# The head-pair loop rotated, and buffers moved to multiples of 512 bytes, in a two-layer decoder trunk

## The chip, the core and the metric

The kernel runs on one core of a Trainium2 chip. The metric is the device time of one launch in microseconds (us), as the median of several runs. A profile is one execution, taken by the hardware profiler. Its engines are PE (TensorE matmuls), PEld (TensorE weight loads), DVE (VectorE), ACT (ScalarE), POOL (GpSimd) and SP (SyncE, which here issues the DMAs).

## What is computed

`x` has 512 tokens of 1024 channels in float32. Each of two layers computes two token mixers from one projection, merges them, and adds a squared-ReLU MLP:

```python
def hybrid_layer(x, g_mix, w_in, w_a, w_b, w_o, g_ffn, w_up, w_down):
    proj = rmsnorm(x, g_mix) @ w_in
    qa, ka, va, qr, kr, vr, gr, ga, gb = jnp.split(proj, SPLIT_POINTS, axis=-1)
    # A: softmax attention, 8 heads of 64 in 3 groups of dilation 1, 4, 16; partial rotary;
    #    the groups' outputs are combined by their softmax denominators
    y_a = combine(outs, lses) @ w_a
    # B: retention, 4 heads of key dim 128 and value dim 256, full rotary, decay per head
    ret = retention(rotary(qr), rotary(kr), vr)
    ret = ret * lax.rsqrt(jnp.mean(ret * ret, axis=-1, keepdims=True) + NORM_EPS)
    y_b = (jax.nn.silu(gr) * ret) @ w_b
    x = x + (sigmoid(ga) * y_a + sigmoid(gb) * y_b) @ w_o
    return x + jnp.square(jax.nn.relu(rmsnorm(x, g_ffn) @ w_up)) @ w_down
```

A last RMSNorm follows the second layer.

## The kernel before

**Units.** All weights stream through SBUF in units of 1 MB (512 KB for a `w_a` unit). SP loads a unit into `raw[s]` as two DMAs, ACT rounds it to `w_hi` (line 393, called by `ahead`), DVE subtracts to get `w_lo` (line 683, `lo`), and PE multiplies. There are two slots of each buffer. To reach float32 precision, activations are also kept as `_hi` and `_lo` parts, and each product is three matmuls in fp32r format (lines 1075 to 1077): `w_hi` by hi, `w_hi` by lo, `w_lo` by hi. A normal unit is two output tiles `o` (PSUM banks `pj[0]`, `pj[1]`) of 8 contraction steps `k`: 48 matmuls that each stream 512 columns of the activation past 128 columns of weights. A `w_a` unit has 4 steps and so 24 matmuls.

**A layer** has 82 units:
- 6 value units (lines 1124 to 1126), in which the activation is the stationary side and 512 columns of weights stream: 288 matmuls in a layer;
- 24 units of the head-pair loop: 4 pairs of 6 units. Units 0 to 2 are queries and keys of the three attention groups, unit 3 those of retention, unit 4 the retention values (lines 1234 to 1236: 96 matmuls that stream 256 columns of weights), unit 5 the swish gate;
- 16 units of `gates(p)`, p = 0 to 3: gate A and gate B (activation `h`), `w_b` (activation `z_hi`, `z_lo`), `w_a` (activation `y_hi`, `y_lo`);
- 4 units of `w_o` (activation `m_hi`, `m_lo`);
- 32 units of the MLP: 16 with activation `h_hi`, `h_lo`, and 16 with `u_hi`, `u_lo`, which are the `z_hi`, `z_lo` buffers again.

So over both layers 88 units of 48 matmuls stream `h` (4224), and 2496 matmuls stream z, m or y: 1920 from `z`, 384 from `m`, 192 from `y`. The attention and retention products themselves are plain fp32 matmuls.

**Places of the buffers.** `x`, `h_hi`, `h_lo`, the raw and split weights follow one another from where the framework's constants end, byte 16512 of each partition. Their sizes are multiples of 2048, so each starts 128 bytes past a multiple of 512. The zone behind the fixed buffers starts at the next multiple of 64, byte 131648, which is 64 bytes past a multiple of 512; `z`, `U`, `m_hi`, `m_lo`, `z_hi`, `z_lo`, `y_hi`, `y_lo`, `ST`, `prob` and others lie in it, all 64 past.

**The pair loop.** PE does units 0 to 2 of the pair, then 12 steps `s` of half a tile of units 3 to 5, with pieces of the attention and retention between them: `scores(j)`, `turn(b)` (transposes of the probabilities), `values(b)`, `st(j)`, `ret(e)`. Each `b` goes PE scores, DVE `masked`, ACT `exp`, PE `turn`, ACT `probT_out`, PE `values`. At the end come `ret(1)` and one matmul by ones, whose result ACT takes the root of (line 544) and DVE inverts (line 856) before it scales two tiles of `z` (lines 861, 864). Only behind these does DVE's queue go on with the next pair: `lo` of its unit 1, then `rotary` (lines 766 to 775) of its units. `rotary` for unit 3 is placed among `masked`. ACT copies each query or key tile from PSUM (`rot_in`, line 465, 467 to 469), which frees the bank; POOL multiplies it by the cosine (line 663).

**After the last pair** PE does `gates(0)`: unit gate A, unit gate B, then `turn_two(0)`, which transposes `U` and waits for `u_scale(0)` and `u_scale(1)` on DVE (line 907), then the `w_b` unit, which waits for each split part of `z`. DVE's order there is `lo`, `gate(0,0,0)`, `factors` (lines 887 to 899), `u_scale(0)`, `u_scale(1)`, `gate(0,0,1)`, and only then the splits of `z` (line 869) and the rest. Each engine runs its own instructions in the order written; all the order between engines is by semaphores.

Of the kernel before, what the change touches and what calls it, by code (L numbers as in the profile page):

```python
# [35 lines left out]
P = 128  # L36
F32 = mybir.dt.float32
# [14 lines left out]
def trunk(nc, a):  # L52
# [30 lines left out]
    with ExitStack() as ctx:  # L83
# [9 lines left out]

        x = sb("x", [P, KT, S], F32)
# [8 lines left out]
        decay = sb("decay", [P, S], F32)  # L103
        mask = sb("mask", [P, S], F32)
        ident = sb("ident", [P, P], F32)
        ones = sb("ones", [P, P], F32)
        inv_d = sb("inv_d", [P, 1], F32)
        gains = sb("gains", [P, 2 * DEPTH + 1, KT], F32)
        gain = sb("gain", [P, 2, KT], F32)
        std = sb("std", [P, 2 * TB], F32)  # L110
        rstd = sb("rstd", [P, 2 * TB], F32)
        eps = sb("eps", [P, 1], F32)

        stats = sb("stats", [P, 2 * TB, 2, HEADS], F32)
        other = sb("other", [P, 2 * TB, 2, HEADS], F32)
        tick = sb("tick", [P, 1], F32)
        warm = sb("warm", [P, 1], F32)


        zone0 = -(-nc.sbuf_base // 64) * 64  # L120
# [24 lines left out]
        nmax = at("P", "nmax", [P, 2 * TB, 2], F32)  # L145
        den = at("P", "den", [P, 2 * TB, 2], F32)
# [7 lines left out]
        y_lo = at("G", "y_lo", [P, KA, S], F32R)  # L154
        sA = at("G", "sA", [P, 2, S], F32)
        sB = at("G", "sB", [P, 2, S], F32)
# [22 lines left out]
        rb = ps("rb", S)  # L179

# [205 lines left out]
        def _(act):  # L386
# [56 lines left out]
            with act.Fori(0, DEPTH) as l:  # L443
# [7 lines left out]
                with act.Fori(0, PAIRS) as i:  # L451
                    J = l * PAIRS + i
                    n = l * LU + P0 + i * P_U
                    q = banks(l, P0, P_U, i, 0)

                    def tile(u, o):
                        act.wait_ge(mm_done, (n + u) * 2 + o + 1 + MM_CREDIT)

                    def rot_in(u, o):

                        t = 2 * u + o
                        tile(u, o)
                        act.wait_ge(rot_out, J * 8 + t + 1)
                        if u < GROUPS:
                            nc.scalar.copy(rot[:], pj[o][:]).then_inc(bank_free[o], 1)  # L465
                        else:
                            nc.scalar.copy(rot[:], pj[o][:])
                            nc.scalar.copy(swp[0:64, :], pj[o][64:128, :])
                            nc.scalar.copy(swp[64:128, :], pj[o][0:64, :]).then_inc(bank_free[o], 1)

                    def exp(b):

                        for side in range(2):
                            act.wait_ge(att_masked, (J * 8 + b) * 2 + side + 1)
                            c, at_ = keys(side, b), side * TB + b // 2
                            nc.scalar.activation(prob[:, c], prob[:, c], ACT.Exp, scale=-1.0,  # L476
                                                 bias=nmax[:, at_, b % 2:b % 2 + 1],
                                                 accum_out=den[:, at_, b % 2:b % 2 + 1]).then_inc(att_exp, 1)

                    def probT_out(b):  # L480
                        act.wait_ge(att_turned, J * 8 + b + 1)
                        if b >= 1:
                            act.wait_ge(att_pv, J * 8 + b)
                        c = slice(keys(0, b).start, S)
                        nc.scalar.copy(probT[:, c], pt[:, c]).then_inc(att_probT, 1)

                    for u in range(GROUPS):
                        ahead(l, P0, P_U, i, u)
                        rot_in(u, 0)
                        rot_in(u, 1)  # L490
                    ahead(l, P0, P_U, i, 3)
                    exp(0)
                    rot_in(3, 0)
                    probT_out(0)
                    exp(1)
                    probT_out(1)
                    exp(2)
                    ahead(l, P0, P_U, i, 4)
                    rot_in(3, 1)
                    probT_out(2)  # L500
                    exp(3)
                    probT_out(3)
                    exp(4)

                    def vR_out(o):
                        tile(4, o)
                        if o == 0:
                            act.wait_ge(ret_mm, J * 2 + 1 + 1)
                        for half in range(2):
                            b = 2 * o + half  # L510
                            mm = nc.scalar.activation(vR[:, b, :], pj[o][:, half * RV:(half + 1) * RV], ACT.Copy,
                                                      scale=rstd[:, b:b + 1])
                        mm.then_inc(bank_free[o], 1)

                    vR_out(0)
                    probT_out(4)
                    exp(5)
                    probT_out(5)
                    exp(6)
                    ahead(l, P0, P_U, i, 5)  # L520
                    vR_out(1)
                    probT_out(6)
                    exp(7)
                    probT_out(7)

                    def ret_square(e):
                        act.wait_ge(ret_out, J * 2 + e + 1)
                        nc.scalar.activation(sqR[e], rb[:],
                                             ACT.Square).then_inc(ret_sq, 1)

                    def gate_sig(o):

                        act.wait_ge(bank_free[o], q + 6 + BANK_CREDIT)
                        nc.scalar.activation(sigR[o], silu[:, o, :], ACT.Sigmoid).then_inc(g_sigmoid, 1)

                    sigR = [swp[:], prob[:, 0:S]]
                    sqR = [rot[:], probT[:, 0:S]]
                    ret_square(0)
                    gate_sig(0)
                    act.wait_ge(att_pv, J * 8 + 8)  # L540
                    ret_square(1)
                    gate_sig(1)
                    act.wait_ge(ret_mean, J + 1)
                    nc.scalar.activation(probT[:], rb[:], ACT.Sqrt, bias=eps[:], scale=1.0 / RV).then_inc(ret_std, 1)

# [9 lines left out]
                ahead(l, G0, G_U, 0, 0)  # L555
# [14 lines left out]
                gate(0, 0, 0)  # L570
                act.wait_ge(z_done, l * KT + KT)
                split_z(range(0, 4))
                gate(0, 0, 1)
                ahead(l, G0, G_U, 0, 1)
                split_z(range(4, 8))
# [92 lines left out]
        def _(dve):  # L668
# [60 lines left out]
            with dve.Fori(0, DEPTH) as l:  # L729
# [23 lines left out]
                with dve.Fori(0, PAIRS) as i:  # L753
                    J = l * PAIRS + i
                    n = l * LU + P0 + i * P_U
                    q = l * LQ + i * P_U

                    def rotary(u, o):

                        t = 2 * u + o  # L760
                        dve.wait_ge(bank_free[o], q + u + 1 + BANK_CREDIT)
                        if t == 0:
                            dve.wait_ge(tables_done, l + 1)
                        if u < GROUPS:
                            nc.vector.memset(tick[:], 0.0)
                            nc.vector.stream_shuffle(swp[:], rot[:], SHUFFLE).then_inc(rot_swap, 1)  # L766
                            dve.wait_ge(rot_swap, J * 6 + t + 1)
                        nc.vector.tensor_tensor(swp[:], swp[:], sinA if u < GROUPS else sinR,  # L768
                                                ALU.mult).then_inc(rot_sin, 1)
                        dve.wait_ge(rot_sin, J * 8 + t + 1)  # L770
                        dve.wait_ge(rot_cos, J * 8 + t + 1)
                        if u == 0:
                            nc.vector.tensor_tensor(qk[:, t, :], rcos[:], swp[:], ALU.add).then_inc(rot_out, 1)
                        elif u < GROUPS:
                            nc.vector.tensor_tensor(qk[:, t, :].rearrange("p (r m) -> p r m", r=4),
                                                    by_residue(rcos[:]), by_residue(swp[:]),
                                                    ALU.add).then_inc(rot_out, 1)
                        else:
                            nc.vector.tensor_tensor(qkR[:, o, :], rcos[:], swp[:], ALU.add).then_inc(rot_out, 1)

                    def masked(b):

                        for side in range(2):
# [594 lines left out]
```

## Time and profile before

| | us |
|---|---|
| median of 3 runs | 2015.46 (2014.9 to 2018.23) |
| the profiled execution's own time | 2016.15 |
| its span, first to last instruction | 2014.3 |
| PE busy | 1987.7 (99%) |
| PEld busy | 1656.1 (82%) |
| DVE busy | 1108.2 (55%) |
| ACT busy | 727.5 (36%) |
| POOL busy | 98.2 (5%) |
| mean DMA rate | 88 GB/s |

1.85 us of the profiled execution lie outside the span, and the median is 0.7 us below that execution. Matmuls are pipelined, and the ends of their rows are modelled, so the busy time of PE is no measure of its speed: the distance from the start of one matmul to the start of the next is.

### The profile page before, as it was taken

The numbers are of one execution on the slowest core, as the hardware profiler recorded it, in microseconds if no ns is written. First come the engines' busy times: TensorE is split into PE (matmuls) and PEld (weight loads), VectorE is DVE, ScalarE is ACT, GpSimd is POOL, SyncE is SP. The second block draws the span as 40 slices with busy tenths as digits, with TensorE's granted clock in tenths as the row PEclk, the third lists the DMA queues.
The fourth block names the chain that finished last, engine by engine and source line by source line (L and its number), as shares of the span: only waits on it lengthen the run. The fifth ranks groups of instructions, "written<-read, shape, count | busy, mean of one in ns | idle before, by whom it ended". The sixth has DMA issues, their size and how long they took to land.

```text
span 2014.3 us, 27151 instructions
## 1 busy us (share of the span) xinstructions
PE 1987.7 (99%) x9640; PEld 1656.1 (82%) x9640; DVE 1108.2 (55%) x1724; ACT 727.5 (36%) x1147; POOL 98.2 (5%) x71
## 2 busy tenths in 40 slices
PE   8999999999999999999999999999999999999999
PEld 7988888888888888888889888888888888888887
DVE  5466574747446635444635574757564565445355
ACT  4143535354223313223322534344432233223233
POOL 0010110200000000000001110202000000000000
PEclk9999999999999999999999999999999999999999
DMA  5321222212223233232333222213133323232321
GB/s 173 106 90 48 83 89 62 89 44 84 94 94 105 84 104 101 87 104 84 105 106 89 63 89 62 89 42 99 44 95 97 111 84 105 84 104 83 104 84 63
DMA packets 202544, 177.63 MB, mean 88 GB/s; under 512 B 8432, under 2 KB 192880, under 8 KB 202224
## 3 DMA queue, kind: packets, MB, share of 16 engines
q1 hardware_dynamic: 202192, 176.51, 27.8%
q8 instruction: 38, 0.62, 0.1%
q10 hardware_dynamic: 288, 0.28, 0.0%
q14 instruction: 26, 0.21, 0.0%
HBM read 174.54 MB, written 2.23 MB: 88 GB/s over the span
## 4 chain that ended last, share of the span: by engine, by line
PE 75%; DVE 14%; issue 7%; ACT 2%; POOL 1%; DVEq 0%; DMA 0%; ACTq 0%; POOLq 0%; SPq 0%
PE pj L1075 19%; PE pj L1077 19%; PE pj L1076 19%; DVE w_lo L683 4%; DVE swp L768 3%; PE yo L1184 2%; DVE swp L766 2%; PE rb L1210 2%; DVE probT L856 1%; PE pj L1234 1%; PE pj L1236 1%; PE pj L1235 1%; PE pt L1171 1%; PE sc L1124 1%; PE sc L1126 1%
## 5 line engine op out<-in xcount | busy, mean ns | idle before, releaser
L1075 PE MATMUL pj<-h_hi,w_hi 128*128 128x512 f32 x1408 | 558.2, 396 | 2.2 <-DVE sA L914 1.6
L1077 PE MATMUL pj<-h_hi,w_lo 128*128 128x512 f32 x1408 | 548.6, 390 | 0.0
L1076 PE MATMUL pj<-h_lo,w_hi 128*128 128x512 f32 x1408 | 548.4, 389 | 0.0
L393 ACT CAST w_hi<-w_raw 128x1024 fp32r<-128x1024 f32 x330 | 329.0, 1045 | 380.1 <-PE pj L1077 286.1
L683 DVE TENSOR_TENSOR w_lo<-w_raw,w_hi 128x1024 fp32r<-128x1024 f32 x330 | 404.4, 1267 | 82.7 <-ACT w_hi L393 82.0
L1075 PEld LDWEIGHTS pj<-h_hi,w_hi 128*128 128x128 f32 x1408 | 264.4, 188 | 61.8 <-DVE w_lo L683 5.5
L1077 PEld LDWEIGHTS pj<-h_hi,w_lo 128*128 128x128 f32 x1408 | 264.3, 188 | 56.1
L1076 PEld LDWEIGHTS pj<-h_lo,w_hi 128*128 128x128 f32 x1408 | 264.5, 188 | 54.9 <-issue 1.8
L1075 PE MATMUL pj<-z_hi,w_hi 128*128 128x512 f32 x640 | 252.6, 395 | 0.6 <-DVE sB L914 0.6
L1077 PE MATMUL pj<-z_hi,w_lo 128*128 128x512 f32 x640 | 252.2, 394 | 0.0
L1076 PE MATMUL pj<-z_lo,w_hi 128*128 128x512 f32 x640 | 252.2, 394 | 0.0
L978 DVE TENSOR_TENSOR x<-pj,x 128x512 f32<-128x512 f32 x80 | 55.2, 691 | 201.4 <-PE pj L1077 201.4
L663 POOL TENSOR_TENSOR rcos<-rot,tables 128x512 f32<-128x512 f32 x64 | 97.7, 1526 | 1307.1 <-ACT rot L465 1175.9
L1075 PEld LDWEIGHTS pj<-z_hi,w_hi 128*128 128x128 f32 x640 | 119.7, 187 | 30.3 <-issue 1.1
L1077 PEld LDWEIGHTS pj<-z_hi,w_lo 128*128 128x128 f32 x640 | 119.7, 187 | 29.8
L1076 PEld LDWEIGHTS pj<-z_lo,w_hi 128*128 128x128 f32 x640 | 119.7, 187 | 29.3
L992 DVE TENSOR_TENSOR relu<-relu,rstd_all 128x512 f32<-128x512 f32 x64 | 44.3, 692 | 90.4 <-ACT relu L607 89.8
L465 ACT COPY rot<-pj 128x512 f32<-128x512 f32 x48 | 28.2, 587 | 182.1 <-PE pj L1077 96.8
L476 ACT ACTIVATE prob<-prob,nmax 128x256 f32<-128x256 f32 (+1 forms) x128 | 62.4, 489 | 66.0 <-DVE nmax L790 65.6
L607 ACT ACTIVATE relu<-pj 128x512 f32<-128x512 f32 x64 | 38.3, 599 | 129.2 <-PE pj L1077 129.2
L1234 PE MATMUL pj<-w_hi,h_hi 128*128 128x256 f32 x256 | 79.4, 310 | 0.0
L790 DVE CUSTOM_DVE_ANT_0 prob<-sc,mask 128x256 f32<-128x256 f32 (+1 forms) x128 | 46.9, 404 | 56.6 <-issue 56.6
(185 smaller groups left out, 2358.1 us busy)
## 6 DMA issues: line engine op xcount, KB each, us to landing
w_raw<-in_w_in SPq DMA_DIRECT2D x152, 512.0 KB, 4.4
w_raw<-in_w_up SPq DMA_DIRECT2D x64, 512.0 KB, 4.4
w_raw<-in_w_down SPq DMA_DIRECT2D x64, 512.0 KB, 4.3
w_raw<-in_w_b SPq DMA_DIRECT2D x16, 512.0 KB, 4.0
w_raw<-in_w_o SPq DMA_DIRECT2D x16, 512.0 KB, 4.0
w_raw<-in_w_a SPq DMA_DIRECT2D x16, 256.0 KB, 3.0
x_nat<-in_x SPq DMA_DIRECT2D x2, 1024.0 KB, 7.0
tables<-in_tables SPq DMA_DIRECT2D x2, 1024.0 KB, 6.8
```

Source lines behind the costliest of these rows:

```text
L393: nc.scalar.copy(w_hi[s][:, c], raw[s][:, c]).then_inc(hi_done, 1)
L476: nc.scalar.activation(prob[:, c], prob[:, c], ACT.Exp, scale=-1.0, bias=nmax[:, at_, b % 2:b % 2 + 1], accum_out=den[:, at_, b % 2:b % 2 ...
L663: nc.gpsimd.tensor_tensor(rcos[:], rot[:], cosA if u < 3 else cosR, ALU.mult).then_inc(rot_cos, 1)
L683: nc.vector.tensor_tensor(w_lo[s][:, c], raw[s][:, c], w_hi[s][:, c], ALU.subtract).then_inc(lo_done, 1)
L768: nc.vector.tensor_tensor(swp[:], swp[:], sinA if u < GROUPS else sinR, ALU.mult).then_inc(rot_sin, 1)
L790: nc.vector.tensor_tensor_reduce(out=prob[:, c], in0=sc[:, (b % 2) * S + c.start:(b % 2) * S + c.stop], in1=mask[:, c], scale=-(DH ** -0.5 ...
L978: nc.vector.tensor_tensor(x[:, t, :], pj[o][:], x[:, t, :], ALU.add).then_inc(bank_free[o], 1)
L992: nc.vector.tensor_tensor(relu2[:, o, :], relu[:, o, :], rstd_all[:], ALU.mult).then_inc(relu_scaled, 1)
L1075: nc.tensor.matmul(out, w_hi[s][:, wc], acts[0], start=first, stop=False)
L1076: nc.tensor.matmul(out, w_hi[s][:, wc], acts[1], start=False, stop=False)
L1077: return nc.tensor.matmul(out, w_lo[s][:, wc], acts[0], start=False, stop=last)
L1234: nc.tensor.matmul(out, hh, w_hi[sl][:, w], start=(k == 0), stop=False)
```

## The change

**Places.** The small tensors move ahead of `x`, and a filler makes `x` start at a multiple of 512 bytes. The zone starts at a multiple of 512 too. `other` becomes a view of `decay`; `sB` and `sA` change places. All streamed operands now start at multiples of 512.

```diff
+        fill = -nc.sbuf_base % 512
+        if fill:
+            sb("fill", [P, fill // 4], F32)
         x = sb("x", [P, KT, S], F32)
...
+        other = decay[:, 0:2 * TB * 2 * HEADS].rearrange("p (b w h) -> p b w h", b=2 * TB, w=2)
...
-        zone0 = -(-nc.sbuf_base // 64) * 64
+        zone0 = -(-nc.sbuf_base // 512) * 512
...
+        sigR = [qkR[:, 0, :], prob[:]]
+        sqR = [qkR[:, 1, :], probT[:]]
```

**Order.** On each engine the loop over pairs becomes: queries and keys of pair 0; then for i = 0 to 2 `attend(i)` followed by the queries and keys of pair i + 1, with the end of pair i between them; then `attend(3)`, whose end lies among `gates(0)`. On PE:

```diff
-                        if 3 <= s < 11:
-                            values(s - 3)
-                        if 2 <= s < 10:
-                            turn(s - 2)
-                        if s % 2 == 1 and s < 8:
-                            scores(s // 2)
-                        if 5 <= s < 9:
-                            st(s - 5)
-                        if 9 <= s < 11:
-                            ret(s - 9)
-                    pe.wait_ge(ret_sum, J + 1)
-                    pe.wait_ge(ret_out, J * 2 + 2)
-                    nc.tensor.matmul(rb[:], ones[:], rcos[:], start=True, stop=True).then_inc(ret_mean, 1)
+                        if s >= 5:
+                            values(J, s - 5, off)
+                        if s >= 4:
+                            turn(J, s - 4)
+                        if s % 2 == 1 and 3 <= s < 10:
+                            scores(J, (s - 3) // 2)
+                        if 6 <= s < 10:
+                            st(J, s - 6)
+                        if s == 10:
+                            ret(i, 0)
...
+                queries_keys(0)
+                with pe.Fori(0, PAIRS - 1) as i:
...
+                    attend(i, off)
+
+                    def last_values():
+                        values(J, 7, off)
+                        ret(i, 1)
+
+                    queries_keys(i + 1, (last_values, lambda: ret_ones(J)))
...
+                attend(PAIRS - 1, off_last)
...
+                gates(0, (lambda: turn_two(0), lambda: turn_two(2)),
+                      (last_of_layer, lambda: ret_ones(l * PAIRS + PAIRS - 1)))
```

The two functions of `queries_keys` run behind the first and the second output tile of unit 0. On DVE, `attend` and what stands between two of them:

```diff
+                def attend(i):
...
                     lo(n + 4, 0)
-                    masked(0)
-                    rotary(3, 0)
-                    masked(1)
-                    masked(2)
-                    masked(3)
+                    rotary(i, 3, 0)
+                    masked(J, 0)
+                    rotary(i, 3, 1)
+                    masked(J, 1)
                     lo(n + 5, 1)
-                    rotary(3, 1)
...
+                    masked(J, 6)
+                    st_decayed(J, 3)
+                    gate_scale(i, 0)
+                    masked(J, 7)
+                    ret_copy(i, 0)
+                    gate_scale(i, 1)
+                    silu_gate(J, 0)
+                    lo(n + 7, 1)
+                    silu_gate(J, 1)
+                    u_copy(i)
+                    ret_copy(i, 1)
+                    ret_add(J)
...
+                    attend(i)
+                    rotary(i + 1, 0, 0)
+                    rotary(i + 1, 0, 1)
+                    ret_inverse(J)
+                    lo(n + 8, 0)
+                    ret_scale(i, 0)
+                    rotary(i + 1, 1, 0)
+                    ret_scale(i, 1)
+                    rotary(i + 1, 1, 1)
+                    lo(n + 9, 1)
+                    rotary(i + 1, 2, 0)
+                    rotary(i + 1, 2, 1)
+                attend(PAIRS - 1)
...
                 g0 = l * LU + G0
-                lo(g0 + 1, 1)
                 gate(0, 0, 0)
+                split_z(range(0, 4))
+                gate(0, 0, 1)
+                ret_inverse(l * PAIRS + PAIRS - 1)
+                ret_scale(PAIRS - 1, 0)
+                ret_scale(PAIRS - 1, 1)
+                split_z(range(4, 6))
+                lo(g0 + 2, 0)
+                gate(0, 1, 0)
                 factors()
                 u_scale(0)
                 u_scale(1)
-                gate(0, 0, 1)
+                split_z(range(6, 8))
+                gate(0, 1, 1)
                 u_scale(2)
                 u_scale(3)
-                split_z(range(0, 4))
-                lo(g0 + 2, 0)
-                gate(0, 1, 0)
-                split_z(range(4, 8))
-                gate(0, 1, 1)
```

On ACT, the end of a pair and the start of the next, and the start of `attend`:

```diff
+                    ahead(l, P0, P_U, i, 3)
+                    rot_in(i, 3, 0)
+                    exp(J, 0)
+                    rot_in(i, 3, 1)
+                    ahead(l, P0, P_U, i, 4)
+                    probT_out(J, 0)
+                    exp(J, 1)
...
+                    ahead(l, P0, P_U, i + 1, 0)
+                    gate_sig(i, 1)
+                    act.wait_ge(att_pv, J * 8 + 8)
+                    ret_square(J, 1)
+                    rot_in(i + 1, 0, 0)
+                    ret_root(J)
+                    rot_in(i + 1, 0, 1)
...
+                gate(0, 0, 0)
+                act.wait_ge(z_done, l * KT + KT - 2)
+                split_z(range(0, 4))
+                ret_root(l * PAIRS + PAIRS - 1)
+                split_z(range(4, 6))
+                gate(0, 0, 1)
+                ahead(l, G0, G_U, 0, 1)
```

No matmul is added or removed, and the programs of POOL and SP keep their order.

## Rows read from the trace of the kernel before

**Rows 1.** The page: busy time of PE, and the chain of waits by engine.

```profile
PE 1987.7 (99%) x9640; PEld 1656.1 (82%) x9640; DVE 1108.2 (55%) x1724; ACT 727.5 (36%) x1147; POOL 98.2 (5%) x71
PE 75%; DVE 14%; issue 7%; ACT 2%; POOL 1%; DVEq 0%; DMA 0%; ACTq 0%; POOLq 0%; SPq 0%
```

**Rows 2.** Groups by line: count | busy, mean ns | idle before, releaser.

```profile
L1075 PE MATMUL pj<-h_hi,w_hi 128*128 128x512 f32 x1408 | 558.2, 396 | 2.2 <-DVE sA L914 1.6
L1075 PE MATMUL pj<-z_hi,w_hi 128*128 128x512 f32 x640 | 252.6, 395 | 0.6 <-DVE sB L914 0.6
```

**Rows 3.** Timeline of PE (start, us, line), `h` streaming: 36 matmuls, then the next.

```profile
180.38 0.39 PE L1075 MATMUL pj<-h_hi,w_hi 128*128 128x512 f32 x1
...
188.31 0.39 PE L1077 MATMUL pj<-h_hi,w_lo 128*128 128x512 f32 x1
188.83 0.50 PE L1075 MATMUL pj<-h_hi,w_hi 128*128 128x512 f32 x1
```

**Rows 4.** Timeline of PE, `z` streaming: the first of 25 matmuls and the last.

```profile
512.18 0.39 PE L1075 MATMUL pj<-z_hi,w_hi 128*128 128x512 f32 x1
...
517.78 0.39 PE L1075 MATMUL pj<-z_hi,w_hi 128*128 128x512 f32 x1
```

**Rows 5.** Timeline of PE, 256 columns of `w` streaming: first of 19 and last.

```profile
136.55 0.28 PE L1234 MATMUL pj<-w_hi,h_hi 128*128 128x256 f32 x1
...
138.71 0.28 PE L1234 MATMUL pj<-w_hi,h_hi 128*128 128x256 f32 x1
```

**Rows 6.** Timeline of PE: 1-column matmuls; 512 columns of `w` streaming, first of 4, last.

```profile
1021.63 2.00 PE L1058 MATMUL rb<-inv_d,ssum 128*128 128x1 f32 x8
...
1024.50 0.63 PE L1126 MATMUL sc<-w_hi,h_lo 128*128 128x512 f32 x1
...
1025.78 0.63 PE L1126 MATMUL sc<-w_hi,h_lo 128*128 128x512 f32 x1
```

**Rows 7.** Busy time in that stretch: PE, PEld, DVE, ACT, POOL, clock, DMA share, GB/s.

```profile
1023.40:1026.80 3.40, 3.40 (x11) 2.74 (x11) 2.78 (x7) 2.26 (x3) 0.00 (x0) 0.55 0.01 4
```

**Rows 8.** Timeline of PE, plain fp32 transposes of `U` in `turn_two(0)`.

```profile
469.54 0.60 PE L1260 MATMUL yo<-ident,U 128*128 128x128 f32 x4
469.98 0.60 PE L1262 MATMUL yo<-ident,U 128*128 128x128 f32 x4
```

**Rows 9.** Timeline of PE in one pair, around `turn(1)` and `st(0)`.

```profile
223.11 0.78 PE L1184 MATMUL yo<-vA,probT 128*128 x6
224.22 0.55 PE L1171 MATMUL pt<-ident,prob 128*128 128x128 f32 x3 [0.33 <-ACT prob L476]
...
234.06 1.15 PE L1161 MATMUL sc<-qk 64*128 64x256 f32 x12
235.89 1.10 PE L1197 MATMUL rb<-qkR 128*128 128x512 f32 x2 [0.69 <-DVE qkR L779]
```

**Rows 10.** Busy time in one pair, columns as in rows 7.

```profile
180.36:270.07 89.71, 88.56 (x501) 74.08 (x500) 55.37 (x107) 39.52 (x77) 12.47 (x8) 1.00 0.24 73
```

**Rows 11.** Timeline of DVE: one `rotary`, first and last instruction.

```profile
282.36 0.76 DVE L766 STREAM_SHUFFLE swp<-rot 128x512 f32<-128x512 f32 x1
...
284.42 0.69 DVE L773 TENSOR_TENSOR qk<-rcos,swp 128x512 f32<-128x512 f32 x1
```

**Rows 12.** Timeline of DVE behind the last pair of layer 0.

```profile
449.34 3.35 DVE L856 RECIPROCAL probT<-probT 128x512 f32<-128x512 f32 x1 [1.31 <-ACT probT L544]
...
455.40 2.35 DVE L683 TENSOR_TENSOR w_lo<-w_raw,w_hi 128x1024 fp32r<-128x1024 f32 x2
...
458.27 0.21 DVE L887 TENSOR_TENSOR fac<-stats,other 128x64 f32<-128x64 f32 x1
...
460.72 2.49 DVE L907 TENSOR_TENSOR U<-U,fac 128x512 f32<-128x512 f32 x4
...
466.14 2.48 DVE L869 TENSOR_TENSOR z_lo<-z,z_hi 128x512 fp32r<-128x512 f32 x4
```

**Rows 13.** Timeline of ACT there: a table load.

```profile
447.33 1.28 ACT L544 ACT_TABLE_LOAD   x1
```

More of the change, by code:

```diff
@@ L449, in _ @@
                 ahead(l, V0, V_U, GROUPS - 1, 1)
[L451 to L542, printed above, removed]
@@ new lines, in exp @@
+                def exp(J, b):
+                    for side in range(2):
+                        act.wait_ge(att_masked, (J * 8 + b) * 2 + side + 1)
+                        c, at_ = keys(side, b), side * TB + b // 2
+                        nc.scalar.activation(prob[:, c], prob[:, c], ACT.Exp, scale=-1.0,
+                                             bias=nmax[:, at_, b % 2:b % 2 + 1],
+                                             accum_out=den[:, at_, b % 2:b % 2 + 1]).then_inc(att_exp, 1)
@@ new lines, in masked @@
+                def masked(J, b):
+                    for side in range(2):
+                        if side == 0:
+                            dve.wait_ge(att_qk, J * 8 + b + 1)
+                            if b >= 1:
+                                dve.wait_ge(att_turned, J * 8 + b)
+                            nc.vector.memset(tick[:], 0.0)
+                        c, at_ = keys(side, b), side * TB + b // 2
+                        nc.vector.tensor_tensor_reduce(
+                            out=prob[:, c], in0=sc[:, (b % 2) * S + c.start:(b % 2) * S + c.stop],
+                            in1=mask[:, c], scale=-(DH ** -0.5), scalar=3e38, op0=ALU.add, op1=ALU.min,
+                            accum_out=nmax[:, at_, b % 2:b % 2 + 1]).then_inc(att_masked, 1)
@@ L866, in split_z @@
+                attend(PAIRS - 1)
                 def split_z(ks):
@@ new lines, in ret @@
+                def ret(i, e):
+                    J = l * PAIRS + i
+                    if e == 0:
+                        pe.wait_ge(st_out, J * TB + TB + 1)
+                        for o in range(2):
+                            pe.wait_ge(bank_free[o], l * LQ + i * P_U + 5 + BANK_CREDIT)
+                    else:
+                        pe.wait_ge(ret_out, J * 2 + 1)
+                        pe.wait_ge(ret_sq, J * 2 + 1)
+                    for j in range(TB):
+                        w = S - j * P
+                        mm = nc.tensor.matmul(rb[:, j * P:S], vR[:, j, e * P:(e + 1) * P],
+                                              ST[:, st0[j]:st0[j] + w], start=(j == 0), stop=(j == TB - 1))
+                    mm.then_inc(ret_mm, 1)
@@ L1142, in _, with ret_ones, attend @@
+                def ret_ones(J):
+                    pe.wait_ge(ret_sum, J + 1)
+                    pe.wait_ge(ret_out, J * 2 + 2)
+                    nc.tensor.matmul(rb[:], ones[:], sqR[0], start=True, stop=True).then_inc(ret_mean, 1)
+                def attend(i, off):
                     J = l * PAIRS + i
@@ L1214, in _ @@
-                    for u in range(GROUPS):
-                        unit(n + u, q + u, u % 2, h)
                     for s in range(12):
```

392 lines of the change are left out of this document (220 added, 172 removed).

## The prediction

> **What bounds the kernel now.** I read the page first. PE is busy 99% of the span and holds 75% of the chain of waits; DVE holds 14% of it [rows 1]. So only three things can move the time: how fast PE takes its stream of matmuls, how long it stands still, and how fast it is clocked. The groups by line show that it hardly stands still: the largest group of all, 1408 matmuls, has 2.2 us of idle time before it [rows 2]. The busy time hides the speed, though, because the ends are modelled. I therefore read the timeline of PE by starts. The reader is to see two speeds for the same instruction at the same clock. With `h` streaming, 36 matmuls start within 188.31 - 180.38 = 7.93 us, 226.6 ns from one to the next [rows 3]. With `z` streaming, 24 steps take 5.60 us, 233.3 ns each [rows 4]. The weights, the shapes and the PSUM banks are alike; what differs is where the streamed operand starts: 128 bytes past a multiple of 256 for `h`, 64 past for `z`. Streaming 512 columns at 2.4 GHz would take 213.3 ns, so `h` pays 13.3 ns and `z` 20.0. With 256 columns of `w` streaming, which also starts 128 past, 18 steps take 2.16 us, 120.0 ns each, where 256 columns would take 106.7: again 13.3 [rows 5]. The extra goes by the start and not by the length.
>
> **What the extra is.** In units of one fp32 column, `h` starts 32 columns into a 256-byte block and pays 32; `z` starts 16 in and pays 48. [...] And plain fp32 transposes, which take two cycles a column, take 0.44 us for four of 128 columns, 110 ns each where 106.7 would be the least, though their operands start 64 and 128 past [rows 8]. These rows also show a small cost that stays, about 3 ns a matmul. An aligned fp32r matmul should then be bound by the array again: 213.3 + 2.7 = 216.0 ns for 512 columns and 109.6 for 256.
>
> [...]
>
> **The change part by part.** All sums are against the span of 2014.3.
>
> *Places.* `h`: 4224 matmuls x (226.6 - 216.0) = 44.8 us. z, m and y, all 64 past: 2496 x (233.3 - 216.0) = 43.2. The 768 that stream 256 columns (8 pairs x 96): x (120.0 - 109.6) = 8.0. The 576 of the value stage have a strided stationary side in two groups of three, and that may bind instead; their gain lies between 0 and 576 x 10.6 = 6.1, and I take 2 as most of them have the stride. Sum: **-98.0 us**. All of it is on PE's own stream. The cover is enough: in a pair DVE is busy for 55.4 of 89.7 us and ACT for 39.5, and DMA engines for 24% [rows 10]. Whether DVE or ACT run otherwise with aligned operands no row shows. Their 512-column steps take 0.69 us; a tenth either way would stay off the path.
>
> *Order, within the pairs.* Three stalls of PE go. At the start of a pair's unit 1 it waits for `lo`, which is queued behind the inverse: 188.83 - 188.31 = 0.52 in place of 0.23, so 0.29 [rows 3], at the 6 junctions between pairs. At `turn(1)` six matmuls of about 0.1 are followed 1.11 us later by the transposes: 0.49. At `st(0)`, which waits for a `rotary` placed behind other work, 0.69 idle plus the modelled end, 0.75 [rows 9]. The last two occur in 8 pairs. Sum 6 x 0.29 + 8 x 1.24 = 11.7. `st(0)` is relieved, since `rotary` of unit 3 now stands ahead of `masked(1)`. `turn(1)` isn't: `masked(1)` waits behind a `rotary` as before, and PE comes a little earlier; 8 x 0.4 = 3.2 return. The cast for unit 5 now stands ahead of `probT_out(0)` on ACT, in the time in which ACT would wait for that `rotary`; without that cover it would cost 1 us. Between pairs DVE gets this queue: rotary 2.75 [rows 11], inverse 3.35, `lo` 2.35, a scale 1.4, rotary, scale, rotary, `lo` [rows 12]. Counted from the end of the ones matmul, `lo` of unit 2 has its first half by 8.8 us, and PE wants it at 48 x 0.216 = 10.4; `lo` of unit 3 has it by 19.5, wanted at 20.8; `rotary` of unit 2 is done by 26.8, wanted at 31. Each fits with 1 to 4 us over. The matmul by ones, `ret(1)` and `values(7)` only move. Sum **-8.5 us**. If the margins fail, up to 1.5 us at each of 6 junctions and 1 us in each of 8 pairs come on top.
>
> *Order, behind the last pair.* Here `factors` and `u_scale` have moved far back in DVE's queue. PE's path: the ones matmul ends at 0, unit gate B ends at 10.4, then `turn_two(0)` wants `u_scale(0)` and `(1)`. DVE's path: ACT's root is ready at about 1.5 (`split_z` and a table load of 1.28 stand before it [rows 13], then 0.69). Then inverse 3.35, four scale steps of 0.69, two splits 1.25, `lo` 2.35, a gate step 0.69, `factors` 460.72 - 458.27 = 2.45, two `u_scale` 2.49 [rows 12]: 15.3 in all, so done at 16.8, the first half at 15.6. Two transposes of 0.88 follow; `w_b` can start at 17.7 instead of 12.2. That is a new stall of 5.5 us per layer, in place of 2.2 us for both layers (1.6 and 0.6 [rows 2]): 11.0 - 2.2 = **+8.8 us**. Queued behind the waiting transposes on PE is everything else. SP's exchange of `stats` waits for `u_copy`, now 7 us later; its result is there before DVE asks, and the `w_a` load behind it has 20 us.
>
> *Clock.* A stretch in which PE has only matmuls of one column is followed by one at half clock [rows 6, 7], in which a matmul takes 427 instead of 227 ns. A stall of 5.5 us may do the same once per layer: 3.4 us at half speed cost 1.7. No row shows a stall of this length, so the bounds are 0 and 3.4 for both; I take **+3.4**, since there a shorter stretch of little work, 2.0 us, came before the fall.
>
> Sum: 2014.3 - 98.0 - 8.5 + 8.8 + 3.4 = 1920.0. With the 1.85 us outside the span 1921.9, and 0.7 less for the median: **1921 us**, 4.7% faster.
>
> **The rivals.**
> *Only equal places count.* `h` and `w` both start 128 past and `z` doesn't match `w`; if the extra 16 cycles of `z` come from that and 32 are a fixed cost of fp32r, all go to 226.7: 2496 x 6.7 = 16.7 us. The half-clock rows speak against a fixed cost. Time: 2015.5 - 16.7 - 8.5 + 8.8 + 3.4 = 2002.
> *Places don't count at all,* and `z` is slower for another reason, so that this half of the change doesn't do what it says: 2015.5 + 3.7 = 2019. [...]
> [...]
>
> **How the numbers follow.** The block reading with the array as the next bound: 0.80. Equal places only: 0.09. No effect of places: 0.05. The spare block always: 0.03. Others 0.03, most of them faster. Within the first case the low end has no 2.7 ns left over (6720 x 2.7 = 18), 4 more from the value stage and no clock loss (3.4): 1895. The high end has stalls of 9 + 8 us at the margins and 7 more behind the last pair: 1945. This range leaves out the other cases, 0.2 in all. About 0.2%, 4 us, is what a measurement of this kernel can tell from no change. Faster: the first two cases and 0.02, so 0.91. Within it: most of the third, 0.04. Slower: 0.05.
>
> **What would show it.** Starts of matmuls 216 ns apart with `h`, and the same with `z`; 240 or 226.7 mean a rival. No idle time before `st(0)`, little at unit 1, and one gap of some 5 us before the transposes of `turn_two(0)` in each layer, perhaps with half clock behind it. The prediction is wrong if starts don't change, or if DVE's `lo` becomes the releaser of units 2 and 3 in the pairs.

## The result, and the profile after

The changed kernel takes **2000.57 us** (median of 4 runs, 1999.23 to 2003.56) where the kernel before takes 2015.18 beside it (4 runs): ratio 0.9927, 95% interval 0.991 to 0.9944. So it is 0.7% faster. I had predicted 1921 us and a range up to 1945, so the time lies some 56 us above the range; it is where one of the rivals, "only equal places count", had put it (2002).

The page of the changed kernel: its first line, busy time of PE, the chain of waits by engine, and the two groups that answer to [rows 2].

```profile
span 1999.1 us, 27115 instructions
PE 1974.0 (99%) x9640; PEld 1663.7 (83%) x9640; DVE 1102.9 (55%) x1724; ACT 730.9 (37%) x1149; POOL 90.8 (5%) x71
PE 82%; DVE 10%; issue 4%; ACT 2%; POOL 1%; DVEq 0%; DMA 0%; ACTq 0%; POOLq 0%; SPq 0%
L1128 PE MATMUL pj<-h_hi,w_hi 128*128 128x512 f32 x1408 | 560.3, 398 | 0.0
L1128 PE MATMUL pj<-z_hi,w_hi 128*128 128x512 f32 x640 | 249.9, 390 | 0.0
```

PE's busy time fell by 13.7 us and its share of the chain rose: the kernel is bound by the same stream as before. The idle times of [rows 2] are gone. The mean of `h` didn't fall (396 before), that of `z` did (395 to 390); the pitch, the time from one start to the next, says it exactly. The timeline of PE (start, us, line), first and last of 32 matmuls with `h`, of 16 with `z`, and of 23 that stream 256 columns of `w`:

```profile
189.61 0.39 PE L1129 MATMUL pj<-h_lo,w_hi 128*128 128x512 f32 x1
...
196.64 0.39 PE L1130 MATMUL pj<-h_hi,w_lo 128*128 128x512 f32 x1
...
474.04 0.39 PE L1128 MATMUL pj<-z_hi,w_hi 128*128 128x512 f32 x1
...
477.44 0.39 PE L1128 MATMUL pj<-z_hi,w_hi 128*128 128x512 f32 x1
```

```profile
136.71 0.28 PE L1294 MATMUL pj<-w_lo,h_hi 128*128 128x256 f32 x1
...
139.35 0.28 PE L1295 MATMUL pj<-w_hi,h_lo 128*128 128x256 f32 x1
```

`h`: 7.03 us for 31 steps, 226.8 ns each, where [rows 3] had 226.6. `z`: 3.40 for 15, 226.7 ns, where [rows 4] had 233.3. 256 columns: 2.64 for 22, 120.0 ns, as in [rows 5]. So 256 columns more take 106.7 ns more, 0.417 ns a column: one column a cycle at 2.4 GHz. Nothing runs at the 216.0 or 109.6 ns that I had forecast. The new pitch of z, m and y alone is worth 2496 x (233.3 - 226.7) = 16.5 us, and the kernel gained 14.6.

The waits of PE (us in total, times, longest), first of the kernel before, then of the changed one, without those of its start:

```profile
PE rb L1197 <- DVE qkR L779: 5.3, 8, 0.7
PE pt L1171 <- ACT prob L476: 2.6, 8, 0.3
PE pj L1075 <- DVE sA L914: 1.6, 2, 0.8
PE pj L1075 <- DVE sB L914: 0.6, 2, 0.3
```

```profile
PE yo L1337 <- DVE U L957: 8.4, 2, 4.2
```

Waits of 10.1 us were taken away and one of 8.4 was made, once per layer. It stands where the text had put it. The timeline of PE behind the last pair of layer 0, and of DVE in the same stretch:

```profile
463.68 0.39 PE L1130 MATMUL pj<-h_hi,w_lo 128*128 128x512 f32 x1
468.26 1.12 PE L1337 MATMUL yo<-ident,U 128*128 128x128 f32 x4 [4.19 <-DVE U L957]
469.17 1.06 PE L1339 MATMUL yo<-ident,U 128*128 128x128 f32 x4
...
472.16 0.63 PE L1129 MATMUL pj<-z_lo,w_hi 128*128 128x512 f32 x1
472.58 0.63 PE L1130 MATMUL pj<-z_hi,w_lo 128*128 128x512 f32 x1
```

```profile
461.59 2.35 DVE L702 TENSOR_TENSOR w_lo<-w_raw,w_hi 128x1024 fp32r<-128x1024 f32 x2
463.86 0.68 DVE L964 TENSOR_TENSOR sB<-pj,rstd_all 128x512 f32<-128x512 f32 x1
464.46 0.21 DVE L937 TENSOR_TENSOR fac<-stats,decay 128x64 f32<-128x64 f32 x1
...
466.90 2.50 DVE L957 TENSOR_TENSOR U<-U,fac 128x512 f32<-128x512 f32 x4
```

PE's last gate matmul starts at 463.68 and the transposes at 468.26: 4.58 us, of which 0.23 are the matmul, so a stall of 4.35. Behind it four transposes take 0.91 (469.17 - 468.26), twice the 0.44 of [rows 8], and `z` matmuls stand 0.42 apart. The windows of the changed kernel show why: from 466.90, still inside the stall, to 473.70 the granted clock is 0.50, half speed, while in a pair it is 1.00. At half speed 512 columns take 427 ns [rows 6], 0.83 ns a column, 1.2 GHz by the same count. A pair, and the stretch from 466.90 (us, then PE, PEld, DVE, ACT, POOL busy, clock, DMA share, GB/s):

```profile
187.13:275.47 88.34, 88.24 (x502) 74.23 (x501) 54.62 (x106) 39.51 (x76) 11.36 (x8) 1.00 0.25 74
466.90:473.70 6.80, 5.44 (x21) 5.06 (x22) 6.79 (x12) 3.02 (x5) 0.00 (x0) 0.50 0.26 91
```

A pair takes 88.34 us where [rows 10] had 89.71 from and to the corresponding point.

### The profile page after: what moved, and what is told of

Same layout as the page of the kernel before. It is cut to its first block, busy times and chain, and to the rows that moved or that the text cites. A ratio compares the mean times of both kernels' runs of the same rounds, so it can differ in the third digit from the quotient of the medians.

```text
span 1999.1 us, 27115 instructions
## 1 busy us (share of the span) xinstructions
PE 1974.0 (99%) x9640; PEld 1663.7 (83%) x9640; DVE 1102.9 (55%) x1724; ACT 730.9 (37%) x1149; POOL 90.8 (5%) x71
## 4 chain that ended last, share of the span: by engine, by line
PE 82%; DVE 10%; issue 4%; ACT 2%; POOL 1%; DVEq 0%; DMA 0%; ACTq 0%; POOLq 0%; SPq 0%
PE pj L1128 21%; PE pj L1129 21%; PE pj L1130 21%; DVE w_lo L702 3%; DVE swp L783 2%; PE yo L1234 2%; PE rb L1261 2%; DVE swp L781 1%; DVE probT L852 1%; PE sc L1211 1%; PE pt L1221 1%; PE sc L1177 1%; PE sc L1179 1%; PE sc L1178 1%; PE rb L1247 1%
## 5 line engine op out<-in xcount | busy, mean ns | idle before, releaser
L702 DVE TENSOR_TENSOR w_lo<-w_raw,w_hi 128x1024 fp32r<-128x1024 f32 x330 | 398.0, 1247 | 95.0 <-ACT w_hi L401 94.2
L682 POOL TENSOR_TENSOR rcos<-rot,tables 128x512 f32<-128x512 f32 x64 | 90.3, 1411 | 1297.6 <-ACT rot L465 1218.2
L783 DVE TENSOR_TENSOR swp<-swp,tables 128x512 f32<-128x512 f32 x64 | 69.2, 1081 | 23.0 <-ACT swp L469 21.4
```

What stands on the lines that cost most here:

```text
L682: nc.gpsimd.tensor_tensor(rcos[:], rot[:], cosA if u < 3 else cosR, ALU.mult).then_inc(rot_cos, 1)
L702: nc.vector.tensor_tensor(w_lo[s][:, c], raw[s][:, c], w_hi[s][:, c], ALU.subtract).then_inc(lo_done, 1)
```

## The experiments

### The two halves of the change, each alone

The change can be taken apart. First the places without the order: the kernel before, with only its buffers moved (`sA` and `sB`, which no matmul reads, keep their order).

```diff
+        fill = -nc.sbuf_base % 512        # ahead of x, h_hi, h_lo, raw, w_hi, w_lo, ...
...
-        zone0 = -(-nc.sbuf_base // 64) * 64
+        zone0 = -(-nc.sbuf_base // 512) * 512
```

> The kernel before with the new places of the buffers alone; every engine keeps its old order. If the places are worth what the two traces' starts say (2496 matmuls x 6.7 ns = 16.6 us), the time is 2015.2 - 16.6 = 1998.6 us, and the starts of z, m and y matmuls are 226.7 ns apart. Rival (the places bring nothing and the whole gain is the order's): 2015.

Measured: 2000.64 us (1997.77 to 2000.98) beside 2016.96, ratio 0.9917 (0.9904 to 0.9931). The timeline of PE has `z` at 226.7 ns (471.77 to 475.17, 15 steps), and the waits of the old order are all there, the two largest of them below:

```profile
471.77 0.39 PE L1078 MATMUL pj<-z_hi,w_hi 128*128 128x512 f32 x1
...
475.17 0.39 PE L1078 MATMUL pj<-z_hi,w_hi 128*128 128x512 f32 x1
```

```profile
PE rb L1200 <- DVE qkR L782: 5.2, 8, 0.7
PE pt L1174 <- ACT prob L479: 2.4, 8, 0.3
```

So the places alone give 16.3 us, all that the change gives.

Then the order alone. In a first kernel the fixed buffers stay at multiples of 512 bytes and the zone starts 64 past one.

```diff
-        zone0 = -(-nc.sbuf_base // 512) * 512
+        zone0 = -(-nc.sbuf_base // 512) * 512 + 64
```

> The changed kernel with its zone at 64 bytes past a multiple of 512 again: the new order alone. My account of the trace after: each pair is 1.3 us shorter, 8 pairs = -10; the new gap before turn_two(0) is +4.3 us a layer less the 1.1 that went, +6.5; and half-clock stretches behind it cost some 3. So 2015.2 -10 + 6.5 + 3 = 2014.7 us, the same as before within 0.2%. Rival (the order gains what I put down, -8.5 + 8.8 + 3.4 = +3.7): 2019. Rival (the order carries the gain): 2000.

Measured: 2006.53 us (2003.94 to 2007.13) beside 2016.96, ratio 0.9947 (0.9934 to 0.9961). That looked like 10 us for the order, but it isn't the order alone: here `z` starts 64 bytes *after* `w` modulo 512, in the kernel before 64 bytes *before* it. The starts of z, m and y matmuls lie 229.0 ns apart on the mean of this trace, not 233.3; the stretch below has 3.44 us for 15 steps, 229.3:

```profile
474.03 0.40 PE L1128 MATMUL pj<-z_hi,w_hi 128*128 128x512 f32 x1
...
477.47 0.39 PE L1128 MATMUL pj<-z_hi,w_hi 128*128 128x512 f32 x1
```

That pitch alone is worth 2496 x (233.3 - 229.0) = 10.7 us, the whole of the gain. The matmuls alone, further down, show the same effect of the sign. So I ran it again with the old relation of the starts:

```diff
-        fill = -nc.sbuf_base % 512
+        fill = -nc.sbuf_base % 512 + 128
-        zone0 = -(-nc.sbuf_base // 512) * 512
+        zone0 = nc.sbuf_base + 192
```

> The changed kernel with its order kept, and the starts set back to what they were relative to one another: fixed buffers 128 bytes past a multiple of 256, the zone of z, m and y 64 past, so z starts 64 bytes before w, as before. So this is the new order alone. By the relative-start theory z streams at 233.3 ns and h at 226.7, as before. By the trace of the changed kernel the order gives 1.3 us at each of some 7 junctions of pairs and takes 4.35 - 0.6 and 4.35 - 1.2 at the two boundaries and some 3 at half clock: -10 + 7 + 3, so about the time of the kernel before, 2014 to 2018. Rival, the order is worth what I predicted, with its clock term +3.7: 2020. Rival, the order is worth as much as the earlier mixed run suggested if its z gained nothing from its place: 2006.

Measured: 2015.82 us (11 runs, 2013.59 to 2017.68) beside 2015.72 (15 runs), ratio 0.9999 (0.999 to 1.0008). **The order alone is worth nothing**, to within 2 us. In its trace `z` is at 233.3 ns again (3.50 us for 15 steps). From one matmul by ones to the next are 88.28 us, so the pairs keep their gain, and the stall per layer with its half clock is there too (the granted clock is 0.50 from 465.70 to 472.50). The timeline of PE, and its wait:

```profile
185.63 1.02 PE L1268 MATMUL rb<-qkR,ones 128*128 128x512 f32 x2
...
273.91 1.02 PE L1268 MATMUL rb<-qkR,ones 128*128 128x512 f32 x2
...
473.04 0.39 PE L1130 MATMUL pj<-z_hi,w_lo 128*128 128x512 f32 x1
...
476.54 0.40 PE L1130 MATMUL pj<-z_hi,w_lo 128*128 128x512 f32 x1
```

```profile
PE yo L1337 <- DVE U L957: 8.3, 2, 4.2
```

### What the pitch depends on

The theories after the result were three: A, the streamed start must be a multiple of 128 bytes (0 and 128 are alike, 64 is not); B, the streamed start alone counts, by its place in a block of 256 bytes, as the prediction took it, with another floor; C, what counts is the streamed start minus the stationary start. A kernel of matmuls alone, 24 to a group, with each start varied by itself. This one and the three like it below were run once each; the group with equal starts gives 226.7 ns in all four.

```diff
+            run(mov[0], sta[0])
+            run(mov[64], sta[0])
+            run(mov[128], sta[0])
+            run(mov[0], sta[64])
+            run(mov[64], sta[64])
...
```

> This kernel computes nothing of the reference: it copies x to the output and, beside that, runs groups of 24 fp32r matmuls of 512 streamed columns that differ only in where the streamed operand starts (0 to 320 bytes past a multiple of 512) or where the stationary one does. Theory A (a start at a multiple of 128 bytes is free, any other costs 6.7 ns, and 13.3 ns are fixed): starts 0, 128, 256 at 226.7 ns a matmul, 64, 192, 320 at 233.3, and the stationary side's start makes no difference. Theory B (my blocks of 256 bytes, with a floor of 226.7 from somewhere else): start 0 and 256 at 226.7 or less, 128 at 226.7, 192 at 220 hidden under 226.7, 64 and 320 at 233.3, 32 at 236.7. Theory C (what counts is whether streamed and stationary operand start at the same place modulo 512): streamed 64 with stationary 64 at 226.7, streamed 0 with stationary 64 at 233.3.

Measured, the mean pitch of the last ten matmuls of each group, in ns (bytes past a multiple of 512 or 256: streamed / stationary):

| starts | ns | starts | ns |
|---|---|---|---|
| 0 / 0 | 226.7 | 0 / 64 | 233.3 |
| 64 / 0, 320 / 0 | 228.9, 228.6 | 0 / 128 | 231.8 |
| 128 / 0 | 233.3 | 0 / 256 | 226.7 |
| 192 / 0 | 233.3 | 64 / 64 | 226.6 |
| 256 / 0 | 226.7 | 64 / 128 | 233.3 |
| 32, 96, 160, 224 / 0 | 233.4 to 234.2 | 0 / 32, 0 / 96 | 233.3, 234.0 |

The timeline of that kernel, whose groups start one after the other, shows it roughly (the next start less this one, for 24 matmuls, so 5.47 us are 227.9 ns each, where the last ten take 226.7):

```profile
76.43 5.63 PE L108 MATMUL acc<-mov256x,sta0x 128*128 128x512 f32 x24
81.90 5.68 PE L108 MATMUL acc<-mov320x,sta0x 128*128 128x512 f32 x24
...
93.02 5.76 PE L108 MATMUL acc<-mov0x,sta64x 128*128 128x512 f32 x24
98.61 5.78 PE L108 MATMUL acc<-mov0x,sta96x 128*128 128x512 f32 x24
...
115.24 5.64 PE L108 MATMUL acc<-mov64x,sta64x 128*128 128x512 f32 x24
120.72 5.76 PE L108 MATMUL acc<-mov64x,sta128x 128*128 128x512 f32 x24
```

With starts 256 bytes apart a group takes 81.90 - 76.43 = 5.47 us, and both sides 64 past take 5.48; a stationary side alone 64 past takes 5.59. A and B fall: 128 / 0 is slow, 64 / 64 is fast. At the two distances that this kernel has, C holds, and so it does with the sign turned: 0 gives 226.7 ns, 64 after gives 228.9, 64 before gives 233.3. It isn't the whole rule: 128 / 0 and 0 / 128 are the same distance modulo 256 and differ by 1.5 ns. It fits the kernel before: `h` and `w` were equal, `z` was 64 before.

This says that the same places shifted together cost nothing, which the kernel itself can test: the changed kernel with every buffer 64 bytes past.

```diff
-        fill = -nc.sbuf_base % 512
+        fill = -nc.sbuf_base % 512 + 64
-        zone0 = -(-nc.sbuf_base // 512) * 512
+        zone0 = -(-(nc.sbuf_base - 64) // 512) * 512 + 64
```

> The changed kernel with every SBUF buffer 64 bytes past a multiple of 256, streamed and stationary ones alike. If the streamed start minus the stationary start is what counts, every start-to-start time is as in the changed kernel, 226.7 ns for h and z, and the time is 2000 to 2002. If the streamed start itself counts (blocks, or a multiple of 128), h and z go to 233.3 or 240: 6720 x 6.7 = 45 us or more on top, 2046 at the least.

Measured: 2001.56 us (1999.94 to 2003.5) beside 2015.72, ratio 0.9933 (0.9918 to 0.9948), the changed kernel's time. `z` in its timeline of PE, 3.40 us for 15 steps:

```profile
472.99 0.39 PE L1130 MATMUL pj<-z_hi,w_lo 128*128 128x512 f32 x1
...
476.39 0.39 PE L1130 MATMUL pj<-z_hi,w_lo 128*128 128x512 f32 x1
```

Multiples of 512 bytes are not what helps; equal starts are.

### What the remaining 13.3 ns are

> This kernel computes nothing of the reference either: the same frame, with other shapes and formats. It asks to whom the fixed 13.3 ns above 512 columns / 2.4 GHz belong. Theory W (the weight load takes them, 128 columns of fp32r): with 64 stationary columns they fall to about 6.7 (220.0 ns), with 32 to 3.3 (216.7), and bf16, whose weights have half the bytes, pays 6.7 or less. Theory S (each fp32r stream has a fixed start, whatever the weights): 226.7 ns with 128, 64 and 32 stationary columns alike, 173.3 with 384 streamed columns, 120.0 with 256, 66.7 with 128; bf16 and plain fp32 pay about 3 ns as the transposes of the trace did. The 6.7 ns of a start 64 bytes past should show with 512, 256 and 128 fp32r columns and not in plain fp32.

The edit is a list of groups as above, with other shapes and types. Measured: with equal starts 64 stationary columns take 229.5 ns and 32 take 231.5, so it isn't the width of the weights, and theory W falls; 384 streamed columns take 173.3 (160.0 + 13.3) and 256 take 120.0 (106.7 + 13.3); 128 take 111.5, where theory S had 66.7, so the 13.3 don't hold for the short ones; a stride of 4 on the stationary side costs 234.8; 64 rows take 226.7. A streamed start 64 past doesn't cost 6.7 ns at the other lengths: 256 columns take 117.8 with it, less than with equal starts, and 128 take 111.8. bf16 takes 215.9 whether it starts 0, 64 or 32 past, and plain fp32 is alike at 0 and 64 past (the starts of the groups below are 20.60 us apart both times, 429.2 ns for each of the 48 records). The timeline of PE: a bf16 group of 24 takes 127.85 - 122.67 = 5.18 us, 215.8 ns each.

```profile
81.47 20.76 PE L108 MATMUL acc<-movf0x,staf 128*128 128x512 f32 x48
102.07 20.76 PE L108 MATMUL acc<-movf64x,staf 128*128 128x512 f32 x48
122.67 5.34 PE L108 MATMUL acc<-movb0x,stab 128*128 128x512 bf16 x24
127.85 5.34 PE L108 MATMUL acc<-movb64x,stab 128*128 128x512 bf16 x24
```

bf16 is 2.6 ns above the 213.3 of 512 columns at 2.4 GHz, fp32r at its best 13.3. The plain fp32 records are 2.5 ns above 426.7, two cycles for each of their 512 columns; counted so, the 110 ns for 128 columns of [rows 8] are 3 above 106.7.

Is there a start that streams faster than an equal one? A scan in finer steps:

```diff
+            run(mov, sta, m0=1)      # 4 bytes on; then 8, 12, 16, ... to 252
+            run(mov, sta, m0=2, w0=2)
+            run(mov, sta, m0=1, w0=1)
```

> Matmuls alone, in groups of 24 of 512 streamed columns of fp32r with a stationary side at a multiple of 512 bytes; the layers are left out, the output is a copy of x. The streamed start is moved in steps of 4 to 48 bytes, then both sides by 8 and by 4, then the stationary side alone by 8. It looks for a relative start that streams faster than 226.7 ns. If the 13.3 ns over 213.3 are fixed, none does, all lie between 226.6 and 235, and equal starts give 226.7 at 8 and 4 past too. If 226.7 itself is a conflict that a certain distance avoids, some start gives 216.

Measured: none of 25 distances is below 226.6. 28, 60 and 252 bytes are as good as 0 (226.7); 12 gives 228.9, 44 and 104 give 230.0, 4 gives 236.7 and 20 gives 240.0, the slowest. The scan also limits theory C: with both sides 8 past the pitch is 231.0, with both 4 past 237.9. Equal starts were enough in steps of 64 bytes; below that the start itself counts as well, by a rule that these runs don't give.

> Matmuls alone, in groups of 24, all fp32r with equal starts modulo 512 bytes; the layers are left out, the output is a copy of x. It asks what the fixed 13.3 ns over the columns are. If they come of both operands lying near each other in SBUF, a stationary side 16, 32, 64 or 96 KB away gives 216. If they come of writing one PSUM bank again and again, alternate banks give 216. If they are whole 64-column blocks plus a half, 480, 496, 500, 504 and 508 columns all take 226.7 or jump by 26.7; if a fixed 32 cycles, they take (columns + 32) / 2.4: 213.3 at 480, 200.0 at 448, 146.7 at 320.

Again a list of groups. Measured: a stationary side 16, 32, 64 or 96 KB away, in the same buffer, or two in turn, and two PSUM banks in turn: 226.7 each time. 508 columns take 227.1, 504 take 226.7, 500 take 223.3, 496 take 223.4, 480 take 216.6, 448 take 202.6, 320 take 146.7, and 192 take 111.9. Blocks of 64 columns would give steps of 26.7 ns. Instead the extra over columns/2.4 is 13.3 ns at 256, 320, 384 and 512 and 15 to 17 at the six lengths from 448 to 508. **So the 13.3 ns over 512 columns are a cost of each fp32r matmul at full clock that no place, distance, bank or width took away here.** (At 256 columns a start 64 past took 2.2 ns of it away.) What it is stays open, as does why it is missing at half clock [rows 6].

### The stall behind the last pair

The trace names `u_scale`, late in DVE's queue. A version of the changed kernel puts `factors` right behind the first gate step (with its exponentials on ACT there, and its small tile moved to where it can be written that early), gives `u_scale` to POOL, and puts the splits of `z` 4 to 8 behind `lo`:

```diff
                 gate(0, 0, 0)
+                factors()
...
-                factors()
-                u_scale(0)
-                u_scale(1)
+                        nc.gpsimd.tensor_tensor(u, u, f.unsqueeze(3).to_broadcast([P, TB, 2, DH]),
+                                                ALU.mult).then_inc(u_scaled, 1)
```

> The changed kernel, and behind the last pair the factors are computed on DVE right behind the gate steps (with their exp on ACT there), u_scale of all four pairs goes to POOL, and the splits of z 4 to 8 stand behind the lo steps. If the 4.35 us gap before the transposes of turn_two(0) is DVE's queue, and the half clock behind it comes of the gap, both go: 2 x 4.35 + 3.4 to 7 less, so 1988 to 1992. Rival: the wait only moves (POOL is slower at the same step than DVE, or lo of unit 2 is late on DVE): 1998 to 2003.

Measured: **1993.87 us** (1993.62 to 1997.81) beside 2015.72, ratio 0.9898 (0.9883 to 0.9913). That lies between the expected 1988 to 1992 and its rival. The clock of the profiled execution is 0.998 of full speed on the mean, the changed kernel's 0.994; no stretch behind the last pair is at half clock (1.00 from 450 to 480 and from 1420 to 1470). (The one execution of four that took 1997.81 us had 0.995; where it lost the clock no trace shows.) But two smaller stalls came, both for gate steps that now stand late on DVE:

```profile
PE pj L1123 <- DVE sB L963: 3.2, 2, 1.6
PE pj L1123 <- DVE sA L963: 3.0, 2, 1.5
```

```profile
464.76 0.60 PE L1332 MATMUL yo<-ident,U 128*128 128x128 f32 x4
465.20 0.60 PE L1334 MATMUL yo<-ident,U 128*128 128x128 f32 x4
...
468.28 0.49 PE L1123 MATMUL pj<-z_hi,w_hi 128*128 128x512 f32 x1 [1.61 <-DVE sB L963]
```

The transposes take 0.44 again. I then moved those two steps forward:

```diff
                 factors()
-                split_z(range(0, 4))
                 gate(0, 0, 1)
+                split_z(range(0, 4))
                 ret_inverse(l * PAIRS + PAIRS - 1)
                 ret_scale(PAIRS - 1, 0)
+                gate(0, 1, 0)
                 ret_scale(PAIRS - 1, 1)
                 lo(g0 + 2, 0)
-                gate(0, 1, 0)
```

> As boundary_fix, but each gate step stands in DVE's queue at the place where its matmuls are done: gate(0,0,1) ahead of the splits of z, gate(0,1,0) ahead of the last scale and lo of unit 2. In boundary_fix PE waited 1.68 and 1.78 us per layer for these two steps. If that is DVE's order alone, both go: 2 x 3.46 = 6.9 less, 1987. Rival, DVE has too much to do there and the wait moves to lo of unit 2 (w_lo, L710): 1991 to 1994.

Measured: **1993.43 us** (1992.58 to 1994.32) beside 2015.59, ratio 0.9889 (0.9872 to 0.9905): no more than the version above, as its rival said. The wait moved on to `lo` of unit 2, and small ones came behind:

```profile
PE pj L1123 <- DVE w_lo L710: 4.2, 2, 2.1
PE pj L1123 <- DVE sB L975: 0.9, 2, 0.5
PE yo L1332 <- DVE y_sum L932: 0.6, 2, 0.3
```

5.7 us of waits replace 6.2. This fits a DVE that has more to do in this stretch than PE leaves time for, so that its order only chooses who is late; two orders were tried. Both versions beat the kernel before and the changed one, by some 7 us the latter.

## Why the prediction was wrong

**Places, -98.0 predicted, -16.3 measured.** This is the step that failed, and it carried nearly the whole forecast. I read the extra of 13.3, 20.0 and 13.3 ns as a function of the streamed start alone, in blocks of 64 columns, and concluded that an aligned operand leaves 216.0 ns, and 109.6 with 256 columns. Both were my estimates, and no run shows them or such blocks: the lowest pitches of fp32r at full clock were 226.6 ns with 512 columns and 117.8 with 256. The 240 ns to which the prediction gave 0.03 didn't come either; equal starts at multiples of 512 take 226.7. The terms, one by one: `h` -44.8 predicted, 0 measured (it had had equal starts all along); z, m and y -43.2 predicted, -16.5 measured; 256 columns -8.0 predicted, 0 measured; the value stage -2 predicted, 0 measured (its starts lie 233 ns apart on the mean in both kernels).

What the runs show in place of the blocks: the pitch goes by the streamed start against the stationary one, and 13.3 ns stay with equal starts. The three pitches that the blocks met exactly, 226.7, 233.3 and 120.0 ns (544, 560 and 288 cycles), had only two different cases behind them: `h` and the 256 columns were one and the same case, equal starts and 32 cycles more than the columns. A formula with a free choice of block size and of floor fits two cases easily. In the kernel before, the streamed start and its distance from the stationary start changed together, so its rows could not tell these apart; I named that rival and gave it 0.09.

**Half clock as evidence against a fixed cost.** The row was read rightly, 427 ns are 512 cycles of 1.2 GHz without extra [rows 6], but the conclusion wasn't forced: the cost of 13.3 ns is fixed over lengths at full clock and still absent at half clock. Both are true in these traces, and I had taken the second to exclude the first. The plain fp32 transposes with their 3 ns were another type: 3 ns is also what bf16 pays (215.9 at 512 columns) and fp32r doesn't, so rows on one format said nothing on another.

**Order within the pairs, -8.5 predicted.** Right, and a bit too small. The `st(0)` stall and that at unit 1 went; I had let 3.2 return at `turn(1)`, 0.4 a pair, and the idle time there is 0.1 now. By the periods each pair is 89.71 - 88.34 = 1.37 us shorter (with 88.28, 1.4), some 11 in 8 pairs. DVE never became the releaser of units 2 and 3.

**Order behind the last pair, +8.8 predicted.** Right in place, releaser and nearly in size: a stall of 4.35 instead of 5.5 per layer, so 8.7 less the 2.2 that went, +6.5.

**Clock, +3.4 predicted.** Right for the mechanism: the clock falls to half some 3 us into the stall of layer 0 (463.91 to 466.90). In layer 0 the 16 transposes start 468.26 to 471.58 in 3.3 us instead of some 1.75, and the 5 matmuls behind them cost about 1 more; in layer 1 the transposes alone. About 4 us by these rows. In the sum -11 + 6.5 + 4 is near 0, and the experiment with the order alone says 0 within 2 us. The changed kernel also shows half clock behind two norms after its start (0.50 from 658.15 to 661.14 and from 1641.60 to 1644.40), where the kernel before has it behind one [rows 6, 7]; the version with the old places has one there too (0.50 from 1650.56 to 1653.12), and which norm is hit varies between kernels, so I make nothing of it.

**The rival** "only equal places count" had its places right: 2496 x 6.7 ns and 32 cycles fixed for fp32r at 512 columns. That its 2002 us also lies so near is in part luck, since it carried +3.7 us for the order, which measured as 0 within 2.

## What to carry to other kernels

An explanation that fits each row exactly is worth little when fewer rows differ than it has choices; list for each row *every* quantity that changes with the one in question (here the stationary start beside the streamed one) and give the rival that uses the other one a fair chance. For fp32r of 512 streamed columns, try equal starts of the streamed and the stationary operand modulo 256 bytes, at multiples of 64 (226.7 ns here, against 228.9 to 233.3 with 64 bytes between them), before looking for an alignment. When work is moved off one stretch into another, add up the follower's queue there first: the gain in 8 pairs was paid back at 2 boundaries, and reordering the crowded queue only changed who waits.

## What the runs showed of the hardware

- fp32r with 512 streamed columns at full clock: 226.7 ns with equal starts modulo 256 bytes (at multiples of 64), 228.9 with the streamed start 64 after the stationary one, 233.3 with it 64 before; up to 240.0 at 20 bytes. With 256 columns 64 after was the faster, 117.8 against 120.0. bf16 doesn't care (215.9 ns at 0, 32 and 64 past).
- The 13.3 ns over the columns is the same at 256, 320, 384 and 512 columns, and doesn't hang on banks or distance; with 64 stationary columns it was 3 ns more, not less.
- Half clock followed a stall of PE of 4.35 us in both layers in the changed kernel, and none did behind two stalls of 1.5 and 1.6 us, 9 us apart, in the version with `factors` and `u_scale` moved (1.00 from 450 to 480).
- A group of 24 fp32r matmuls of only 32 rows fell to half clock some 3 us after its start at 112.09 (1.00 to 115.30, 0.50 from there), though nothing stood still; 64 rows in another kernel took 226.7 ns. That the few rows are the reason is not shown: the group just ahead of it, 320 columns read with a stride of 2, ran slowly too, 283 ns a matmul. Windows of that kernel (us, PE, PEld, ACT, POOL busy, clock, DMA share, GB/s); the first reaches from that group into this one, the second lies behind the fall:

```profile
110.00:115.00 5.00, 5.00 (x21) 3.58 (x20) 0.00 (x0) 0.00 (x0) 1.00 0.00 0
115.30:119.30 4.00, 4.00 (x11) 2.98 (x10) 0.00 (x0) 0.00 (x0) 0.50 0.00 0
```
